# Two-layer diffusion trunk on one core: PE order of the recurrent branch, and accumulator banks by longest time since last use

## The reference, cut to what matters

```
q-norms, projections  ->  proj = h @ w_in
branch a (rwkv7):  S_t = S_{t-1} * w_t + (S_{t-1} a_t) b_t^T + v_t k_t^T ;  o_t = S_t r_t    (8 heads of 64, forward and backward)
branch b (gla):    chunked gated linear attention, 4 heads, forward and backward
branch c (mla):    softmax attention over 512 own and 256 cached keys, 8 heads
y = (g_a*y_a + g_b*y_b + g_c*y_c) @ w_out ;  x = x + gate*y
```

## Time and profile before

| | us |
|---|---|
| median of 3 runs | 2876.14 (2874.84 to 2878.2) |
| the profiled execution: its time | 2874.18 |
| its span, first to last instruction | 2872.4 |
| PE busy | 2693.6 (94%) |
| DVE busy | 1180.9 (41%) |
| ACT busy | 854.2 (30%) |
| mean granted TensorE clock | 0.984 |

### The profile page before, as it was taken

How to read it: one execution, slowest core, us unless ns; L and a number is a source line. 1 busy time by engine, 2 the same in 40 slices (tenths; PEclk the granted TensorE clock), 3 DMA queues, 4 the chain that set the end, 5 groups by cost and what they waited for, 6 DMA issues and landing times.

```text
span 2872.4 us, 49516 instructions
## 1 busy us (share of the span) xinstructions
PE 2693.6 (94%) x21716; PEld 1726.2 (60%) x21716; DVE 1180.9 (41%) x2329; ACT 854.2 (30%) x1366; POOL 33.8 (1%) x62
## 2 busy tenths in 40 slices
PE   8999999999988999999999999999998899999997
PEld 2585756657555665555555858585755556555554
DVE  1452626454275454211134545454547644421112
ACT  1332314242244444200013232323324444420000
POOL 0000000000000000000000000000000000000000
PEclk9999999999999999999999999999999999999998
DMA  8101011020200100222231010101010010012221
GB/s 324 52 10 68 24 40 52 15 77 2 76 23 23 35 16 23 89 72 67 84 99 59 2 40 9 39 10 32 17 32 23 23 35 15 23 54 67 73 76 62
DMA packets 35844, 140.79 MB, mean 49 GB/s; under 512 B 4592, under 2 KB 4624, under 8 KB 35120
## 3 DMA queue, kind: packets, MB, share of 16 engines
q1 hardware_dynamic: 31968, 116.74, 12.6%
q0 software_dynamic: 3664, 20.88, 2.1%
HBM read 130.62 MB, written 6.98 MB: 48 GB/s over the span
## 4 chain that ended last, share of the span: by engine, by line
PE 82%; DVE 9%; ACT 6%; issue 2%; DMA 1%; POOL 0%; ACTq 0%; DVEq 0%; SPq 0%; POOLq 0%
PE psum L500 79%; PE psum L503 2%; DVE tmp L1401 1%; DVE tmp L1404 1%; DVE m_nm L1876 1%; DVE tmp L1412 1%; ACT tmp L1373 1%; DVE tmp L1578 1%; DVE acts L1401 1%; DVE tmp L1551 1%; ACT tmp L1126 1%; DVE acts L1404 1%; DMA ring<-units 1%; ACT acts L1126 1%; ACT L1121 0%
## 5 line engine op out<-in xcount | busy, mean ns | idle before, releaser
L500 PE MATMUL psum<-hT,ring 128*128 128x128 f32 (+1 forms) x3904 | 1127.2, 443 | 32.4 <-DVE acts L1404 22.6
L500 PEld LDWEIGHTS psum<-hT,ring 128*128 128x128 f32 x3904 | 613.6, 193 | 557.9 <-issue 521.7
L500 PE MATMUL psum<-tmp 64*64 64x64 f32 (+9 forms) x10624 | 706.9, 259 | 56.7 <-DVE tmp L1404 13.9
L500 PEld LDWEIGHTS psum<-tmp 64*64 64x64 f32 (+3 forms) x10624 | 555.6, 149 | 173.0 <-issue 60.5
L1126 ACT ACTIVATE tmp<-psum 128x512 f32<-128x512 f32 (+6 forms) x406 | 214.0, 530 | 570.2 <-PE psum L500 490.5
L500 PE MATMUL psum<-acts,ring 128*128 128x512 f32 (+1 forms) x768 | 210.8, 434 | 0.0
L1126 ACT ACTIVATE acts<-psum 128x640 f32<-128x640 f32 (+4 forms) x206 | 109.4, 531 | 336.5 <-PE psum L500 310.2
L1401 DVE TENSOR_TENSOR tmp<-psum,tmp 128x256 f32<-128x256 f32 (+2 forms) x184 | 75.7, 411 | 263.0 <-PE psum L500 224.7
L1404 DVE TENSOR_TENSOR tmp<-tmp,psum 128x640 f32<-128x640 f32 x32 | 26.3, 821 | 375.4 <-ACT tmp L1391 205.6
L500 PEld LDWEIGHTS psum<-acts,ring 128*128 128x128 f32 x768 | 117.3, 191 | 92.1 <-issue 92.1
L1391 ACT ACTIVATE tmp<-psum 128x640 f32<-128x640 f32 x32 | 22.5, 703 | 443.6 <-PE psum L500 443.6
(11 more groups left out here) (152 smaller groups left out, 1854.4 us busy)
## 6 DMA issues: line engine op xcount, KB each, us to landing
ring<-units SPq DMA_DIRECT2D x218, 512.0 KB, 3.5
small_sb<-small POOLq DMA_DIRECT2D x2, 2944.0 KB, 11.5
hT<-xT POOLq DMA_DIRECT2D x1, 2560.0 KB, 12.6
tmp<-xT POOLq DMA_DIRECT2D x8, 320.0 KB, 4.5
x_keep<-hT POOLq DMA_DIRECT2D x8, 320.0 KB, 4.7
tmp<-x_keep POOLq DMA_DIRECT2D x8, 320.0 KB, 3.5
yT<-acts POOLq DMA_DIRECT2D x8, 320.0 KB, 3.5
tmp<-masks SPq DMA_DIRECT2D x1, 1536.0 KB, 8.8
```

The source lines that it names most:

```text
L500: return nc.tensor.matmul(out, lhsT, rhs, start=start, stop=stop, skip_group_check=True)
```

## The change

1. `ticket` picks, of the free banks (pairs of banks only at even places), those whose last use lies furthest back; the bank takes the ticket's number as its age, a score ticket's 4 more, and a held bank gets its age when it is released.
2. A group's opening: Ab of its first step is issued at the end of the group before, between S/O of step s and U of step s + 1 (for steps 2 and 4); `turns` of the second step comes after both Ab; the first X is issued before Ak, the second behind it.
3. `open_outputs` is split: S is opened before Ya (first step) or before TaT (second step), O before Yb (first step) or before the closing of the step before (second step).
4. At the end of a pair the first item of the next pair (or `kvd`) is issued in two halves of four k-tiles, around `ovar`; `beat(11)` moves ahead of `omean`. The `project` of that item at the pair's start is gone (for pair 0 it stands ahead of the loop), and so is the closing `project` of `kvd`.

```diff
--- before.py
+++ after.py
@@ -390,21 +390,29 @@
         emptied = {"act": act_e, "dve": dve_e}
 
 
-        book = {"at": 0, "last": [None] * 8, "held": set()}
-
-        def ticket(pe, key, banks, by):
-
-
-            at = book["at"]
-            while at + banks > 8 or any(b in book["held"] for b in range(at, at + banks)):
-                at = (at + 1) % 8
+        book = {"n": 0, "age": [0] * 8, "last": [None] * 8, "held": set()}
+
+        def ticket(pe, key, banks, by, late=0):
+
+            book["n"] += 1
+            free = [b for b in range(0, 8, banks) if not book["held"] & set(range(b, b + banks))]
+            at = min(free, key=lambda b: sorted(book["age"][b:b + banks], reverse=True))
             for old, o_by in dict.fromkeys(o for o in book["last"][at:at + banks] if o):
                 for one in o_by.split():
                     pe.wait_ge(emptied[one].sem, emptied[one][old])
             book["last"][at:at + banks] = [(key, by)] * banks
-            book["at"] = (at + banks) % 8
+            book["age"][at:at + banks] = [book["n"] + late] * banks
             values["at", key] = at
             return at * 512
+
+        def hold(at, banks=1):
+
+            book["held"] |= set(range(at // 512, at // 512 + banks))
+
+        def release(at, banks=1):
+
+            book["held"] -= set(range(at // 512, at // 512 + banks))
+            book["age"][at // 512:at // 512 + banks] = [book["n"]] * banks
 
         def place(key):
 
@@ -543,7 +551,7 @@
 
                 if k == 0:
                     grown["at"] = ticket(pe, ("modrow", l, j), 1, "act")
-                    book["held"].add(grown["at"] // 512)
+                    hold(grown["at"])
                 if k % 2 == 0:
                     grown["w"] = unit(2)
                     unit_done()
@@ -551,7 +559,7 @@
                 last = mm(psum[0:2, at:at + 512], sc[:, k, :], grown["w"][:, k % 2, :], k == 0, k == KT - 1)
                 if k == KT - 1:
                     last.then_inc(filled.sem, filled.mark(("modrow", l, j)))
-                    book["held"].discard(at // 512)
+                    release(at)
                 elif k % 2 == 1:
                     last.then_inc(used.sem, used.mark((l, 4 * j + k // 2)))
 
@@ -561,14 +569,14 @@
                 for k in tiles:
                     if k == 0:
                         grown["item_at"] = ticket(pe, key, 2, "dve" if it[0] in GATES else "act")
-                        book["held"] |= {grown["item_at"] // 512, grown["item_at"] // 512 + 1}
+                        hold(grown["item_at"], 2)
                         grown["item_w"] = unit()
                         unit_done()
                     at = grown["item_at"]
                     last = wide(at, grown["item_w"][:, k, :], hT[:, k, :], k == 0, k == KT - 1)
                     if k == KT - 1:
                         last.then_inc(filled.sem, filled.mark(key))
-                        book["held"] -= {at // 512, at // 512 + 1}
+                        release(at, 2)
 
             def mod_turn(l, j):
 
@@ -609,9 +617,9 @@
                 pe.wait_ge(s_small, 16 * (l + 1))
                 pe.wait_ge(act_e.sem, act_e[(l, "wdad", 0)])
                 pe.wait_ge(act_tanh.sem, act_tanh[l])
+                project(l, BESIDE[0][0])
                 for p in range(PAIRS):
 
-                    project(l, BESIDE[p][0])
                     pe.wait_ge(dve_kksq.sem, dve_kksq[l, p])
                     sums(("kkss", l, p), bd, [w_ys], by="dve")
                     for d in range(2):
@@ -681,7 +689,7 @@
 
                         def scores(s, key, kind):
 
-                            at = ticket(pe, (key, l, p, s), 2, "dve")
+                            at = ticket(pe, (key, l, p, s), 2, "dve", 4)
                             for d in range(2):
                                 moving = fac[:, 4 * d + A_:4 * d + R_ + 1, cols(d, s)]
                                 for h in range(2):
@@ -702,20 +710,26 @@
 
                         opened = {}
 
-                        def open_outputs(s):
-
+                        def open_state(s):
+
+                            if s == 3:
+                                return
                             TA, TB = B(s, "TA", 2), B(s, "TB")
                             got(s, ("TB", "act"))
-                            opened["S", s] = ticket(pe, ("S", l, p, s), 1, "dve") if s != 3 else None
-                            for d in range(2) if s != 3 else ():
-                                mm(psum[:, opened["S", s] + P * d:opened["S", s] + P * d + P], TB[:, 2 * d + 1, :],
-                                   TA[:, d, :], d == 0, False)
+                            opened["S", s] = at = ticket(pe, ("S", l, p, s), 1, "dve")
+                            for d in range(2):
+                                mm(psum[:, at + P * d:at + P * d + P], TB[:, 2 * d + 1, :], TA[:, d, :], d == 0, False)
+                            hold(at)
+
+                        def open_output(s):
+
+                            TA = B(s, "TA", 2)
                             opened["O", s] = at = ticket(pe, ("O", l, p, s), 1, "dve")
                             for u in range(4):
                                 d, hs = u // 2, slice(64 * (u % 2), 64 * (u % 2) + 64)
                                 mm(psum[hs, at + P * d:at + P * d + P], TA[:, d, hs], B(s, "ArkT")[:, u, :],
                                    d == 0, False)
-                            book["held"] |= {opened[k, s] // 512 for k in "SO" if opened[k, s] is not None}
+                            hold(at)
 
                         def halves64(s, key, by, second, lhsT_at):
 
@@ -739,14 +753,8 @@
                             return (B(s, "OffX")[64 * c:64 * c + 64, u, 64 - 64 * c:128 - 64 * c],
                                     slice(64 - 64 * c, 128 - 64 * c))
 
-                        for s in steps:
-                            if s in (0, 1, 3):
-                                turns(s)
-                        for s in steps:
-                            scores(s, "Ab", B_)
-                        scores(steps[0], "Ak", K_)
-                        beat(0)
-                        for s in steps:
+                        def untransposed(s):
+
                             pe.wait_ge(dve_XT.sem, dve_XT[l, p, s])
                             at = ticket(pe, ("X", l, p, s), 1, "act")
                             for u in range(4):
@@ -755,6 +763,18 @@
                                     last = mm(psum[cs, at + 64 * u:at + 64 * u + 64], B(s, "XX", 8)[cs, u, :], ident2[cs, :],
                                               True, True)
                             last.then_inc(filled.sem, filled.mark(("X", l, p, s)))
+
+                        if steps[0] == 0:
+                            turns(0)
+                            scores(0, "Ab", B_)
+                        for s in steps[1:]:
+                            scores(s, "Ab", B_)
+                            turns(s)
+                        beat(0)
+                        untransposed(steps[0])
+                        scores(steps[0], "Ak", K_)
+                        for s in steps[1:]:
+                            untransposed(s)
                         for s in steps:
                             got(s, ("X", "act"))
                             XT, X = B(s, "XX", 8)[:, 0:4, :], B(s, "XX", 8)[:, 4:8, :]
@@ -811,7 +831,7 @@
                         for s in steps:
                             got(s, ("V2", "dve"))
                             block(s, "V3", "dve", B(s, "E"), B(s, "G"))
-                        open_outputs(steps[0])
+                        open_state(steps[0])
                         beat(8)
                         for s in steps:
                             got(s, ("V3", "dve"), ("AV", "act"))
@@ -820,10 +840,13 @@
                         for s in steps:
                             got(s, ("Ya", "act"), ("Ya", "dve"))
                             halves64(s, "Ye", "dve", 0, carried)
+                        open_output(steps[0])
                         beat(10)
                         for s in steps:
                             got(s, ("Ye", "dve"))
                             halves64(s, "Yb", "act dve", 1, solved)
+                        for s in steps[1:]:
+                            open_state(s)
                         for s in steps:
                             got(s, ("Yb", "act"), ("Yb", "dve"))
                             if s != 4:
@@ -847,9 +870,9 @@
                                 for d in range(2):
                                     mm(psum[:, at + P * d:at + P * d + P], st[:, d, :], F(d, R_, s), False, False)
                                 if s + 1 in steps:
-                                    open_outputs(s + 1)
+                                    open_output(s + 1)
                                 got(s, ("U", "dve"))
-                            at, s_at = opened["O", s], opened["S", s]
```

(15 more changed lines are left out.)

## The result

The changed kernel takes 2832.35 us (median of 4 runs, 2827.66 to 2833.68), the kernel before 2875.49 in the same comparison: a ratio of 0.9848, 95% interval 0.9831 to 0.9865, or 43 us less. I had predicted 2819 with 2795 to 2852: inside the range, the gain smaller than forecast.

A forecast was written before the change was run, and what follows sets the result against it. PE, busy 94% of the span, was taken to bound the kernel. Terms 40 + 5 + 30 - 18 = 57 us off the profiled 2874.18 gave 2817; with the median 2 us above, 2819, range 2795 to 2852.

The forecast's parts named there:

- Gated attention: Filling items, kit and go get banks emptied earlier; 43 us over both layers, net 40, bounds 10 and 47.
- The gap ahead of level 6: Gated attention: 2.5 us PE wait for DVE's factors stays open; 3 us set aside for the lower clock behind it.
- rival (a): Hidden DVE and ACT chains set the gated attention's pace; its banks give 10 instead of 40: 2849, chance 0.14.
- Softmax attention: The new rule removes the bank waits of pt, mostly moved on one operation; 5 us gained, bounds 0 and 15.
- Boundaries: Between pairs the chain behind ovar is exposed, kkss waits about 3.5 us: 8 us late plus 10 clock, cost 18.
- Openings and closings: Recurrent branch: earlier Ab and split openings of S and O save 30 us in all, bounds 15 and 38.
- opening of group (0, 1): Recurrent branch: Ab of step 0 ahead of turns(1) lets DVE's copies start 0.85 us earlier; gain 0.7 a pair.
- the stretch from O of step 3 to O of step 4: Recurrent branch, group (4): Ab out of the way, Ak covers ACT's copy of X; gain 1.25 a pair.
- opening of group (2, 3): Recurrent branch: early Ab of step 2 fills U's bank wait, DVE's copies go on at once; 1.0 a pair.
- layer 0's pairs 1 and 3: Recurrent branch: the 2.50 us wait of Ak of step 2 for Ab's bank shrinks; 3 more each, 6 us.
- rival (d): The new rule picks in effect the old banks, only PE's order counts: 12 us gained, 2864, chance 0.03.
- Rival (c): Early Ab blocks two of eight banks; waits of 3.2 plus 1.7 us at 16 places: 78 us, 2897, chance 0.04.

The follow-up runs named there:

- early_ab4_only: Changed kernel with Ab of step 2 issued again at its group's opening, only Ab of step 4 early: 2822.84 us.
- banks_only: Kernel before the change with only the new bank rule (ticket, hold, release), PE's order as before: 2799.09 us.
- no_late: Changed kernel without the 4 added to a score ticket's age: 2874.44 us.
- item_behind_ovar: Changed kernel with the whole item issued behind ovar instead of four k-tiles ahead of it, beat(11) still ahead of omean: 2818.2 us.
- no_early_ab: Changed kernel with Ab of steps 2 and 4 issued again at its group's opening: 2821.25 us.
- old_boundary: Changed kernel with the pair boundary of before (omean, beat(11), ovar, then the whole item): 2805.47 us.
- wait_filled3: Changed kernel with three unread matmul calls (2.6 us) issued ahead of the wait of each kkss of pairs 1 to 3: 2825.36 us.

## Why the prediction was right or wrong

**Gated attention: right.** The first pass gave 5.7 us in each layer (5.8 forecast), the third 7.0 (7.4), the second 7.5 in layer 0 and 5.0 in layer 1 (7.4), the fourth 0.9 (1.0). In layer 1's second pass level 4 gets the bank of an item just filled and waits 1.76 us, a wait of the old kind that the rule still makes: 2.5 us. Some 0.9 of this is the wait and 1.6 the clock of 0.66 behind it, since `early_ab4_only` has the same wait there at 1.00 and loses only 0.9. The gap ahead of level 6 is 1.35 and not 2.5, and the clock behind it stays at 1.00, so the 3 us set aside for it were not needed. That the sum of 40 was met so closely is in part luck: these 3 us stand against the 2.5 of a wait that it did not have. The lower bound of 10 doesn't follow from its own words either: half of the first pass's gain in each layer is 6. That rival (a)'s hidden chains would cap the gain at 10 is excluded, and the gain was 40. The Trainium skill (TensorE: Matmul & The Clock Gate, "HAM oscillation — how this bites in real kernels") tells of a kernel that gained nothing further from PSUM double-buffering; this kernel is another case: with the same eight banks, the choice of bank alone gave 76 us.

**Softmax attention: right**, 4.4 for 5.

**Boundaries: the mechanism right, the size somewhat low.** The chain from ovar's result to kksq measured 7.56 us (7.6), the wait 3.28 (3.5, though 7.6 less 4.3 is 3.3), the clock 0.50 to 0.64 over the 4 us behind it. With the clock kept up the six kkss are 11.9 us later (8; layer 0 lost 5.3, not 2.1), and the clock took 10.5 (10). 22.4 for 18, inside the bounds.

**Openings and closings: this failed.** 30 us forecast, 19 measured: the recurrent branch as a whole cost 3.7 us, of which 22.4 are the boundaries and 0.3 the last one. The opening of group (0, 1) gave 6.2 with the clock kept up (5.6 forecast) and the stretch from O of step 3 to O of step 4 11.6 (10 and a part of the closings). What is missing lies between O of step 0 and O of step 3: 14 forecast (8 for the opening of group (2, 3), 6 for layer 0's pairs 1 and 3), 1.2 measured. The step is the sentence "Now Ab of step 2 (8 matmuls, 0.87) fills this place, and U starts about where it did." The place is only 0.35 us wide, too small for 0.87; two of the eight pairs don't have it; and it was a wait for a bank, not for data. Under the new rule U has no such wait, and nothing is left to fill. Ab costs its own time ahead of U, and in three pairs it gets the bank of O of step 0 and waits 0.35 us for it besides, so that U comes 1.2 to 1.7 us later than it could. The forecast gain behind U came in full in three pairs only: X2 of step 2 starts 6.3 us behind U of step 1's result instead of 7.3. In four of the others Ab of step 3, X of step 3 or Ak of step 2 waits 0.65 to 1.61 us for a bank.

**What I did not ask** is what each half does alone. I set the new order's savings against the waits of the kernel before; the bank rule removes the same waits by itself. Of the 19 us, `banks_only` has 18. Against it the new order costs 34 us at boundaries and ahead of the first `kit` (clock included) and 9 for the early Ab, and gives 10 by the rest: the 33 us by which the recurrent branch is longer than in `banks_only`. So the order as a whole is slower than no change, which my sum of "30 - 18 = 12" for rival (d) had the wrong way round: order alone is +32.

**Rival (c)** got 0.04, with the age of 4 as the reason. It is a real mechanism and that reason is all that holds it off: `no_late` shows it at 42 us, about half of the price I gave. The long wait strikes once a pair, not at each of the 16 early Ab, and makes 27 of the 42.

## What to carry to other kernels

Ask of each wait that a new order is to fill whether it is for data or for a buffer; a better buffer rule takes the second kind for nothing, and whatever is moved into the place then costs its own time, or takes over the wait. Judge a moved piece by the whole loop, not by the stretch that it left. Where a long chain follows a small operation, issue this first and put all independent work behind it; behind the six waits at the boundaries the lower clock cost nearly as much (10.5 us) as the lateness itself (11.9).

## What the runs showed of the hardware that was not expected

The same wait of PE, ahead of the same matmuls, did not always cost the clock. In `item_behind_ovar` PE waits 1.85 us ahead of ovar in all eight pairs. Over the 4 us behind it the clock stayed at 1.00 (2.4 GHz) in five pairs and was 0.57, 0.60 and 0.65, between 1.2 and 2.4 GHz, in three. The view of busy time by stretch, pair 1 of layer 1 and pair 1 of layer 0:

```profile
1794.30:1798.30 4.00, 4.00 (x14) 2.29 (x15) 0.00 (x0) 2.59 (x3) 0.00 (x0) 1.00 0.01 4
```

```profile
425.30:429.30 4.00, 3.96 (x9) 1.96 (x10) 0.00 (x0) 1.64 (x2) 0.00 (x0) 0.57 0.65 264
```

The wait of 1.76 us in the second pass of layer 1's gated attention does the same from kernel to kernel, here in the changed kernel and in `early_ab4_only`; that pass took 44.84 and 43.20 us:

```profile
2189.10:2193.10 4.00, 3.92 (x25) 2.82 (x26) 3.90 (x7) 1.05 (x2) 0.00 (x0) 0.66 0.02 4
```

```profile
2182.70:2186.70 4.00, 3.97 (x34) 2.85 (x36) 3.90 (x7) 0.99 (x2) 0.00 (x0) 1.00 0.02 4
```

Even one of the six waits of 3.28 us at the boundaries of `no_early_ab` has 1.00 behind it (pair 1 to 2 of layer 1), and a wait of 1.38 us in `old_boundary` 1.00 in two pairs and 0.57 in a third. So neither the length of a wait nor the kind of matmuls behind it decides alone, and what does is not shown here. A price for the clock, such as 1.75 us a boundary, is a mean over several waits, and differences of 1 to 2 us between kernels in one stretch can come from it alone.

And a bank rule is sensitive far from where it is changed. One ticket more at each boundary (`wait_filled3`) made O1-O3 3.8 us longer: Ab of step 3 waits 1.38 us for a bank in three pairs instead of one, once with the clock at 0.57 behind it. The first pass of layer 0's gated attention gave 5.7 us in the changed kernel and 4.0 in `banks_only`, with no edit there: in the latter level 4 waits 1.36 us for a bank.
